# Prompt attention: unscaled probabilities, reciprocal sums turned over channels and multiplied into the gate

## What is computed

```python
def window_attend(q, k, v, q_pos, k_pos, sinks):
    s = einsum('bnqhgd,bnshd->bnhgqs', q, k) * ATT_SCALE
    s = s - slopes * dist
    s = where(live, s, NEG)
    p = softmax(concatenate([s, sink], -1), axis=-1)[..., :-1]
    return einsum('bnhgqs,bnshd->bnqhgd', p, v)
...
o = window_attend(qb, band(kb), band(vb), pos, k_pos, sinks).reshape(B, T, -1)
out = (o * silu(gate)) @ w_out
```

## Time and profile before

| | us |
|---|---|
| median of 3 runs | 1608.47 |
| lowest and highest | 1608.23, 1614.58 |
| the profiled execution | 1608.11 |
| its span, first to last instruction | 1606.3 |
| prompt attention, from its first DMA issue to the end of its last gating | 1351.05 to 1491.83 |
| final projection and norm | 1491.9 to 1606.3 |

### The profile page before, as it was taken

The page is one execution under the profiler, slowest core; times in us unless marked ns, Lnnn a source line. Parts: engine busy times, 40 slices in busy tenths (PEclk is TensorE's granted clock), DMA queues, the critical chain, the costliest instruction groups (busy, mean ns, idle before and its releaser), DMA issues. The chain is left out here.

```text
span 1606.3 us, 40134 instructions
## 1 busy us (share of the span) xinstructions
PE 1482.3 (92%) x17472; PEld 1321.9 (82%) x17472; DVE 827.4 (52%) x1646; ACT 616.4 (38%) x1239; POOL 307.4 (19%) x343
## 2 busy tenths in 40 slices
PE   6999999999797799999999977999999997887897
PEld 5989898888797699998999956879999995544686
DVE  7637346777510366666666644472111122886446
ACT  7526357777411122222222314151111132786414
POOL 0000000000000344434534420000000100998000
PEclk9999999999999899999999988999999998899899
DMA  6623223556632644425424116305334344421202
GB/s 217 178 65 99 68 97 109 166 165 213 194 95 56 139 116 95 91 56 145 95 58 94 36 61 233 109 1 180 107 81 100 85 127 127 135 86 50 81 24 88
DMA packets 242383, 173.63 MB, mean 108 GB/s; under 512 B 148607, under 2 KB 218175, under 8 KB 241039
## 3 DMA queue, kind: packets, MB, share of 16 engines
q1 hardware_dynamic: 209063, 155.56, 33.6%
q10 hardware_dynamic: 33152, 15.60, 3.3%
HBM read 110.97 MB, written 60.46 MB: 107 GB/s over the span
## 5 line engine op out<-in xcount | busy, mean ns | idle before, releaser
L329 PE MATMUL mix_acc<-mix_high,mix_w_high 128*128 128x364 f32 (+1 forms) x768 | 181.4, 345 | 18.5 <-DVE mix_w_low L543 12.9
L329 PE MATMUL mix_acc<-mix_low,mix_w_high 128*128 128x364 f32 (+1 forms) x768 | 172.3, 333 | 2.2 <-DVE mix_low L529 2.1
L329 PE MATMUL mix_acc<-mix_high,mix_w_low 128*128 128x364 f32 (+1 forms) x768 | 171.8, 333 | 0.0
L329 PEld LDWEIGHTS mix_acc<-mix_high,mix_w_high 128*128 128x128 f32 x768 | 132.4, 192 | 39.6 <-issue 19.7
L329 PEld LDWEIGHTS mix_acc<-mix_low,mix_w_high 128*128 128x128 f32 x768 | 135.3, 191 | 3.6 <-DVE mix_low L529 3.6
L329 PEld LDWEIGHTS mix_acc<-mix_high,mix_w_low 128*128 128x128 f32 x768 | 135.7, 191 | 0.0
L1927 POOL TENSOR_SCALAR att_score<-att_score,att_sums 128x256 f32<-128x256 f32 (+1 forms) x128 | 110.3, 883 | 119.9 <-DVE att_sums L2049 119.6
L1319 PE MATMUL out_acc<-qkvg_room_r_high,qkvg_room_w_high 128*128 128x364 f32 (+1 forms) x320 | 106.3, 332 | 3.0 <-issue 1.9
L543 DVE TENSOR_TENSOR mix_w_low<-mix_wt,mix_w_high 128x1024 fp32r<-128x1024 f32 x32 | 39.2, 1224 | 134.0 <-ACT mix_w_high L391 133.6
L1319 PE MATMUL out_acc<-qkvg_room_r_high,qkvg_room_w_low 128*128 128x364 f32 (+1 forms) x320 | 105.8, 331 | 0.0
L1319 PE MATMUL out_acc<-qkvg_room_r_low,qkvg_room_w_high 128*128 128x364 f32 (+1 forms) x320 | 105.8, 331 | 0.0
(11 more groups left out here) (254 smaller groups left out, 3493.3 us busy)
## 6 DMA issues: line engine op xcount, KB each, us to landing
mix_wt<-in_w_in SPq DMA_DIRECT2D x32, 512.0 KB, 4.2
qkvg_room_wt<-in_w_att SPq DMA_DIRECT2D x20, 512.0 KB, 4.1
delta_bk<-scr_bk SPq DMA_DIRECT2D x17, 512.0 KB, 4.7
delta_kr<-scr_kr SPq DMA_DIRECT2D x17, 512.0 KB, 7.0
scr_kr<-mix_outs SPq DMA_DIRECT2D x16, 512.0 KB, 3.6
scr_bk<-mix_outs SPq DMA_DIRECT2D x16, 512.0 KB, 4.4
early_xpad<-in_xpad SPq DMA_DIRECT2D x8, 548.5 KB, 7.3
scr_xg<-early_xs SPq DMA_DIRECT2D x8, 544.0 KB, 2.7
```

What stands on the lines that cost most here:

```text
L329: mm = pe.matmul(acc[:, s, k, 0:width], w[:, s, d, :], r[:, d, n0:n0 + width], start=d == 0 and q == 0, stop=d == DT - 1 and q == 2)
```

## The change

Only `attention` changes; its lines move down by a few. The probabilities stay unscaled. The reciprocal sums of a half (8 heads) are repeated by POOL 64 times each into `wide` (128 tokens by 512), four PE transposes (`spread_sums`) turn that into channels by tokens in a bank of `turn`, and DVE multiplies it into the gate (`scale_gate`) before the gate meets `pv` (`gate_half`). `values` now puts even heads in partitions 0 to 63 and odd heads in 64 to 127, in 8 matmuls of 256 columns, so that one multiplication of 128x512 gates a half. The values of all tiles are loaded by one DMA and turned once in tile 0. `turn_probs` fills one bank at a time, and the banks of `turn` are used in strict alternation in the order of `USES`. Of the 8 copies of a tile DVE takes two. The negation is folded into the maximum by `less_sink`. `sums` has a slot for even and one for odd tiles.

```diff
+        USES = [("values", k) for k in range(TILES // 2)]
+        for tile in range(TILES):
+            for group4 in range(KVH):
+                if group4 % 2 == 0:
+                    USES.append(("sums", tile, group4 // 2))
+                USES += [("probs", tile, group4, part) for part in range(len(blocks(tile)))]
...
+        def turn_bank(*use):
+            return turn[:, USES.index(use) % 2, :]
...
+                    if t == 0:
+                        sp.dma_start(v_in[:], scr["av"][0:TILES].rearrange("t p j n -> p t j n")).then_inc(v_loaded, 16)
...
             def _(pool):
...
-                    for g in range(KVH):
-                        pool.wait_ge(inverted, 4 * t + g + 1)
-                        for h in range(4 * g, 4 * g + 4):
-                            pool.tensor_scalar(score[:, t % 2, h, 0:width(t)], score[:, t % 2, h, 0:width(t)], sums[:, h:h + 1], None, ALU.mult).then_inc(normed, 1)
+                    for i in range(2):
+                        pool.wait_ge(inverted, 4 * t + 2 * i + 2)
...
+                        rows = sums[:, t % 2, 8 * i:8 * i + 8].rearrange("p (h o) -> p h o", o=1).broadcast_to([128, 8, 64])
+                        pool.tensor_copy(wide[:, i, :].rearrange("p (h n) -> p h n", h=8), rows).then_inc(widened, 1)
...
+                def wait_for_bank(*use):
...
+                    last = USES[n]
...
+                    elif last[0] == "sums":
+                        pe.wait_ge(gate_scaled, 2 * last[1] + last[2] + 1)
+                    elif by_vector(*last[1:]):
+                        pe.wait_ge(p_kept_too, PROBS_DVE.index(last) + 1)
+                    else:
+                        pe.wait_ge(p_kept, PROBS_ACT.index(last) + 1)
...
+                def spread_sums(b, i):
+                    pe.wait_ge(widened, 2 * b + i + 1)
+                    wait_for_bank("sums", b, i)
+                    for j in range(4):
+                        mm = pe.transpose(turn_bank("sums", b, i)[:, 128 * j:128 * j + 128], wide[:, i, 128 * j:128 * j + 128], ident[:])
+                    mm.then_inc(spread, 1)
+
                 def turn_probs(b, g):
...
+                    pe.wait_ge(raised, 20 * b + 5 * g + 5)
                     for s in range(len(blocks(b))):
+                        wait_for_bank("probs", b, g, s)
...
                     for g in range(KVH):
+                        if t and g % 2 == 0:
+                            spread_sums(t - 1, g // 2)
                         if t:
                             turn_probs(t - 1, g)
+                        if t >= 2 and g == 0:
+                            values(t - 2, 1)
+                        if t and g == 2:
+                            values(t - 1, 0)
                         scores(t, g)
-                        if t and g % 2:
-                            values(t - 1, g // 2)
...
                     for g in range(KVH):
+                        if t and g % 2 == 0:
+                            scale_gate(t - 1, g // 2)
+                        if t >= 2 and g % 2:
+                            keep_probs(t - 1, g)
                         bias_group(t, g)
                         if g:
                             norm_group(t, g - 1)
-                        if t and g % 2:
-                            gate_group(t - 1, g - 1)
-                            gate_group(t - 1, g)
+                        if t >= 2 and g == 0:
+                            gate_half(t - 2, 1)
+                        if t and g == 2:
+                            gate_half(t - 1, 0)
                     norm_group(t, KVH - 1)
```

More of the change, by code:

```diff
@@ L1866, in attention @@
         gate_sample = m.sb("gate_sample", 128, DT, NB * NT)
-        top, low, sums, extra = (m.sb(x, 128, H) for x in ("top", "low", "sums", "extra"))
+        top, low, extra, less_sink = (m.sb(x, 128, H) for x in ("top", "low", "extra", "less_sink"))
+        sums, wide = m.sb("sums", 128, 2, H), m.sb("wide", 128, 2, 512)
         sc = m.ps("sc", 128, 2, 2, 512)
@@ L2010, in _ @@
                             raise_group(t, g - 1)
[L2011 to L2014 removed]
+                    if t == 0:
+                        for k in range(TILES // 2):
+                            act.wait_ge(v_turned, k + 1)
+                            act.activation(v_rows[:, 2 * k:2 * k + 2, :].rearrange("p t n -> p (t n)"), turn_bank("values", k), ACT.Copy).then_inc(v_kept, 1)
                     raise_group(t, KVH - 1)
@@ L2048, in norm_group @@
                     dve.wait_ge(totalled, 4 * t + g + 1)
[L2049 to L2058 removed]
+                    dve.reciprocal(total, total).then_inc(inverted, 1)
```

144 lines of the change are left out of this document (88 added, 56 removed).

## The result

| | before | after |
|---|---|---|
| median of the runs, us | 1610.49 (1608.23 to 1614.58) | 1668.75 (1666.19 to 1673.67) |
| ratio | | 1.0358, 95% interval 1.0337 to 1.0379 |
| profiled execution: its time, its span, us | 1608.11, 1606.3 | 1670.12, 1668.3 |
| mean granted clock of TensorE | 0.964 | 0.948 |
| first scores of tile 0 to last gating, us | 135.3 | 192.5 |

The changed kernel is slower by 58 us. The forecast was 1657, within 1640 to 1673, with a chance of 0.92 for slower. The attention stage is 57.2 us longer. The profiled span is 62.0 us longer, because this execution also came 5.7 us later to the stage, through code that the change doesn't touch, and was 0.9 us shorter behind it; the runs of the kernel before differ by as much among themselves, and the medians don't show those 5.7.

A forecast was written before the change was run, and what follows sets the result against it. The prediction took POOL to set the kernel's period, with DVE close behind. It summed 1608.1 + 32.8 (waits over the stage) + 16.8 (clock) = 1657.7 us, given as 1657, range 1640 to 1673.

The forecast's parts named there:

- So POOL sets the period: Kernel before, attention stage: POOL's 16 multiplications, 14.8 us of a 15.28 us tile, set the period, DVE close behind.
- the wait for the last exponentials: DVE at g = 0: the scaling stands behind the last group's sum, which needs ACT's last four exponentials; 1.8 us idle.
- its clock term: PE's clock falls once at each of seven tile boundaries, 2.4 us each: +16.8 us.
- the first rival: Same waits, but PE's clock holds: only +32.8 us, 1641; chance 0.14.
- both waits of a tile: After each scaling, g = 0 and g = 2, DVE waits out PE's transposes, values and scores: 3.9 us idle, twice a tile.
- a milder stretch: Middle of a tile, PE working 0.53 us in 3.5: no clock fall counted there.
- the second rival: The clock falls at both stalls of each tile: six more falls of 2.4 us, +14.4, 1672; chance 0.17.
- the head: Stage up to tile 2's first scores: tile 1 has the same two waits, +2.8 us.
- five periods: First scores of tile 2 to those of tile 7: 77.2 us before, 108.2 after at 21.65 each, +31.1.
- the tail: From tile 7's first scores to the stage's end: 34.0 us before, 32.9 after, -1.1.
- SP's wait: SP's queue: the gate load waits for a gating, the next tile's queries and keys behind it; costed at nothing.
- the banks don't bind: Rival: scaling early enough that banks and queues don't bind, PE sets a 13.8 us period: -9 us, 1599; chance 0.05.

The follow-up runs named there:

- that order mended: Changed kernel with the same operations in another order on PE and DVE, scores and turns of sums moved ahead, bank use fitted: 1602.50 us, ratio 0.9966.
- the kernel with pairs and loads ahead: Changed kernel reordered in pairs of groups on PE, ACT and DVE, a tile's gate load issued behind the next queries and keys: 1588.79 us, ratio 0.9859.
- the scores first: Changed kernel with even groups' scores on PE moved ahead of the turned probabilities and values: 1628.43 us, ratio 1.0103.
- DVE's move: Changed kernel with the gate scaling by the first half of the sums moved ahead of the last group's sum on DVE: 1642.03 us, ratio 1.0216.

## Why the prediction was right, and where it was off

**The bound of the kernel before: right rows, wrong conclusion.** "So POOL sets the period" rested on 14.8 us of work in 15.28. The run without the multiplications has the same 15.28. It did no harm to the sum, since I stepped the four queues rather than count POOL's work as gained, but it is the sentence on which somebody who wanted this change would rest it. A share of 95% is not yet a cause.

**The mechanism: as forecast.** The scaling on DVE is asked for by PE's transposes, in front of the scores that DVE itself wants next. At full clock DVE idles 3.70 us (forecast 3.9), a period is 21.2 to 21.3 us (21.65), the wait for the last exponentials 1.75 (1.8), PE's stalls 4.05 and 1.91 us (3.8 and 2.2). The kernel with the stalls filled takes 1641.3 us; the forecast's sum without its clock term is 1640.9, the 1641 of the first rival.

**The sizes within it.** The `values` take 1.88 us from start to start, the lower end of what I allowed and not the middle, and splitting them costs nothing. POOL's repeat is 0.64 us, below both bounds (0.92 and 1.6): the nearest rows that I had were all dearer. DVE's operations of 512 columns are 0.67 to 0.69, as the earlier trace rows. The `values`, which lie in both waits of a tile, are 0.34 of the 0.4 us by which the period came out shorter; POOL lies in neither. The forecast's "less 1 for `values` at 1.87" was too little by its own numbers: 2 x 0.18 us a period over five periods are 1.8.

**The clock: the term that was mis-sized.** "The middle of a tile has a milder stretch (0.53 us of work in 3.5) and I count none there" is the step that failed. The clock falls at both stalls, as the second rival had it, and as two stretches and the slow `values` behind both show. In the steady tiles it costs 25.65 - 21.27 = 4.4 us a period where I took 2.4; in the whole 27.4 us, measured by filling the stalls, against 16.8: 10.6 us too little. The waits were 2.0 too much (30.8 against 32.8), and the kernel before has a median of 1610.5 beside this kernel and not the 1608.1 from which the sum started, 2.4; together 11.0 of the 11.8 us by which the forecast was low, and the rest is rounding. Measured against its own runs of the kernel before (1609.0), the filled kernel has 32.3 us of waits, half a microsecond from the forecast, and leaves 26.0 for the clock. The price of one fall, 2.2 us in the mean of a period's two, was about right; the number of falls was 13 and not 7. The second rival, 1672, is off by 3 on the other side.

**The stage by its parts,** from the profiled executions: the head 28.7 us against 24.1 (+4.6, forecast +2.8 and a fall of 2.4, +5.2), five periods 128.3 against 77.2 (+51.1, forecast +31.1 and five falls of 2.4, +43.1), the tail 35.6 against 34.0 (+1.5, forecast -1.1 and a fall, +1.3). So what the profile shows too much lies in the five periods alone. The single DMA of all values landed 6.0 us after its issue, and PE went from tile 0's last scores to turning the values without a wait.

**Costed at nothing.** SP's wait: right for this kernel (2 us, not told from none), and the first thing in the way as soon as the rest was mended. "These are wanted more than a tile later" was a statement on the period that the change itself had made long.

**The rivals.** That the clock holds (1641) is excluded by the stretches, and is what the filled kernel shows. That the banks don't bind (1599, given 0.05) was wrong of this kernel, for the reason given there, the order on DVE; with that order mended, it is 1602.5.

The Trainium skill, page "TensorE: Matmul & The Clock Gate", section on HAM oscillation, says that repeated idle gaps make the clock fall again before each burst. The stretches above agree, 0.57 and 0.51 behind the two stalls; but the gaps of its example are longer than the 1.91 us of the middle, so by itself it doesn't decide on the middle of the tile. The same page of the Trainium skill, "Part 4: PE-mode transpose", says that a transpose doesn't count as busy in the same way. The two together are the second rival, which came out nearer than my count. No run here separates the part on transposes: in the kernel with pairs and loads ahead transposes are 5.3 of PE's 13.28 us and the clock stays at 1.00, but matmuls are never far.

## What to carry to other kernels

Before an engine is asked for a new result in the middle of a loop, follow what that engine is itself waiting for: if its next input stands behind the asker in the other queue, both wait, and the wait is as long as the whole row between. Put the independent work ahead of the one that asks. An engine that is busy 95% of a period may be one of two limits of the same length, and a run that empties it while keeping its instructions (one column instead of 256) tells so for the price of one experiment. And when a stretch gets faster, look again at each wait that was costed at nothing.

## What the runs showed of the hardware that I had not expected

- In the middle of a tile PE was idle for 0.58 us, did four transposes (0.63), was idle for 1.91, and in the tile shown the clock stood at half for the 6.4 us behind that. With an idle time of 0.59 us in the last place (the scores first) it did not fall: the `values` behind it took 1.95. With 1.9 us behind eight transposes (the boundary with DVE's move) it had fallen three times of six, so the last idle time alone doesn't decide it. Filling the stall with matmuls whose result nobody reads made the kernel 27 us faster.
- An idle matmul of 256 columns over all of the array took 0.45 us (8 of them, 16 records, in 3.62 us), while eight of the same columns over half of the array's columns, two side by side, took 1.88.
- POOL copies 8 numbers a partition out to 512 columns in 0.64 us; its multiplication of 256 columns by a scalar takes 0.92 us, and 0.29 us even for one column.
